# Hybrid decoder layer on one core: sink heads' values on two column halves with divided probabilities, 17 early U products, and an earlier place for a tile's exponential on ScalarE

## What is computed

```
proj = x @ w_in
fox  = forgetting attention, 8 heads x 64, causal
swa  = sliding window (128), 8 query heads, 2 key/value heads x 64, rotary, a sink logit per head:
       p = softmax([scores, sink])[..., :-1];  o = p @ v
x = LayerNorm(ALPHA * x + concat(fox, swa) @ w_out)
per token, per head (8): q = x @ w_query; scores of 2 x 128 sub keys; top 16 of each; top 16 of the sums
       g = softmax(best);  h = gelu(expert_u[idx] . x);  y = sum (g * h) * expert_v[idx]
x = LayerNorm(ALPHA * x + y)
```

## Time and profile before

| what | value |
|---|---|
| runs | 2673.73, 2677.02, 2678.19 us (median 2677.02) |
| the profiled execution, its own time | 2682.55 us |
| its span | 2680.7 us |
| PE busy | 2532.4 us, 94% |
| DVE busy | 2277.8 us, 85% |
| ACT, POOL busy | 904.8 us (34%), 1320.4 us (49%) |
| mean granted clock of PE | 0.983 |

### The profile page before, as it was taken

How to read it: one execution, slowest core, us unless ns; L and a number is a source line. 1 busy time by engine, 2 the same in 40 slices (tenths; PEclk the granted TensorE clock), 3 DMA queues, 4 the chain that set the end, 5 groups by cost and what they waited for, 6 DMA issues and landing times.

```text
span 2680.7 us, 45230 instructions
## 1 busy us (share of the span) xinstructions
PE 2532.4 (94%) x16925; PEld 1644.2 (61%) x17115; DVE 2277.8 (85%) x4525; ACT 904.8 (34%) x1602; POOL 1320.4 (49%) x864
## 2 busy tenths in 40 slices
PE   8999979999988888999999999999999999999996
PEld 5566546599877766564564665664664665664652
DVE  3666656669899998788998998998999999999998
ACT  2344345411144556332232232332332332332324
POOL 2110010100044441467777776776676776777762
PEclk9999979999999999999999999999999999999998
DMA  5100323310024477999999999999999999999995
GB/s 220 39 17 17 113 88 130 134 56 27 27 76 128 139 221 247 368 405 375 368 379 367 373 386 365 365 387 367 340 384 375 362 366 379 360 383 368 370 321 220
DMA packets 283584, 697.89 MB, mean 260 GB/s; under 512 B 31192, under 2 KB 113624, under 8 KB 277088
## 3 DMA queue, kind: packets, MB, share of 16 engines
q0 software_dynamic: 110592, 402.70, 39.6%
q1 hardware_dynamic: 170176, 284.77, 29.8%
q10 hardware_dynamic: 2592, 7.47, 0.8%
HBM read 631.51 MB, written 61.24 MB: 258 GB/s over the span
## 4 chain that ended last, share of the span: by engine, by line
PE 44%; DVE 15%; issue 9%; DMA 7%; POOL 2%; ACT 1%; DVEq 0%; SPq 0%; ACTq 0%; POOLq 0%
PE h_psum L1742 18%; PE o_psum L2225 12%; PE g_psum L2225 8%; PE r_t_psum L1203 4%; DMA early<-v_blocks,pick_index 3%; DVE rt_hot L1641 3%; DMA early<-u_rows,pick_index 2%; POOL early L1749 2%; DVE rt_top_u L1486 2%; PE h_psum L1250 1%; DVE early L2066 1%; DVE wide L2070 1%; DVE rt_top L1484 1%; DVE rt_hot L1651 1%; DVE rt_scores L1488 1%
## 5 line engine op out<-in xcount | busy, mean ns | idle before, releaser
L1742 PE MATMUL h_psum<-early 128*128 128x384 bf16 x5448 | 759.0, 299 | 1.2 <-DVE early L1732 0.9
L1742 PEld LDWEIGHTS h_psum<-early 128*128 128x128 bf16 x5448 | 532.5, 98 | 225.4 <-issue 2.1
L1749 POOL DMA_INDIRECT early<-u_rows,pick_index x320 | 466.8, 1459 | 203.1 <-DVE dots L2066 117.6
L1749 POOL DMA_INDIRECT early<-v_blocks,pick_index x320 | 462.6, 1446 | 192.6 <-DVE wide L2070 112.7
L2225 PE MATMUL o_psum<-v_split,w_split 128*128 128x512 bf16 x2293 | 538.4, 379 | 1.4
L2070 DVE SCALAR_TENSOR_TENSOR wide<-early,dots,wide 128x1024 f32<-128x1024 f32 x320 | 405.8, 1280 | 31.5 <-DMA early<-v_blocks,pick_index 28.7
L2066 DVE CUSTOM_DVE_ANT_0 early<-early,wide 128x1024 f32<-128x1024 f32 x320 | 388.1, 1221 | 38.2 <-DMA early<-u_rows,pick_index 35.5
L2225 PEld LDWEIGHTS o_psum<-v_split,w_split 128*128 128x128 bf16 x2304 | 225.7, 98 | 272.4 <-issue 1.1
L2225 PE MATMUL g_psum<-v_split,w_split 128*128 128x512 bf16 x1400 | 344.7, 380 | 17.3 <-DVE wide L2058 4.2
L1944 ACT ACTIVATE v_split<-early 128x512 bf16<-128x512 f32 x256 | 159.4, 624 | 327.7 <-PE o_psum L2225 311.5
L2225 PEld LDWEIGHTS g_psum<-v_split,w_split 128*128 128x128 bf16 x1536 | 150.0, 98 | 176.3 <-issue 12.0
(11 more groups left out here) (235 smaller groups left out, 3224.8 us busy)
## 6 DMA issues: line engine op xcount, KB each, us to landing
early<-v_blocks SPq DMA_DIRECT2D x256, 256.0 KB, 6.3
early<-u_blocks SPq DMA_DIRECT2D x114, 512.0 KB, 7.1
gates<-wide SPq DMA_DIRECT2D x16, 2048.0 KB, 9.7
gate<-gates SPq DMA_DIRECT2D x32, 1024.0 KB, 9.5
early<-w_query SPq DMA_DIRECT2D x8, 1024.0 KB, 5.6
gates_late<-wide SPq DMA_DIRECT2D x4, 2048.0 KB, 8.0
gate<-gates_late SPq DMA_DIRECT2D x32, 256.0 KB, 14.6
early<-w_fox SPq DMA_DIRECT2D x4, 1536.0 KB, 6.5
```

Of the source, the lines that this page charges most:

```text
L1742: mm = pe.matmul(bank(half)[:, 0:width * P], u_split[:, k, part, c], xs[:, first:first + width, xpart, c, :], start=(c == 0 and part == 0 ...
L1749: pool.indirect_dma_start(row, None, source, bass.IndirectOffsetOnAxis(ap=pick_index[:, tile, at:at + 1], axis=0)).then_inc(arrived, 16)
```

## The change

Three edits, and a fourth that follows from the first:

1. In the mix phase the values are made with the 64 columns of values as weights and the turned probabilities moving, a head on either half of the array's columns, so the output arrives turned; `turn_out` and `scale_out` are gone. In their place DVE's `normalise(n)` divides the probabilities before PE turns them: `turn_probs(n)` now waits for `normed` instead of `exp_done`. `normalise(n+1)` stands behind `norm` in DVE's step n.
2. 17 blocks of U products are early instead of 14: three steps of routing hold 32 pieces instead of 16. The early blocks are 6 + 7k instead of 6 + 9k.
3. ACT's `softmax(t-1)` stands behind the second group of scores of tile t instead of the third, and `softmax(0)` inside tile 1 instead of behind it.

```diff
 PRE_AHEAD = 4
-PRE_PIECES = ((0,) * 8 + (1,) * 2 + (2,) * 2 + (3,) * 2 + (4,) * 1 + (0,) * 1,) * (DENSE - 2) + (
+PRE_PIECES = ((0,) * 4 + (1,) * 3 + (2,) * 4 + (3,) * 1 + (4,) * 2 + (5,) * 2,) * (DENSE - 2) + (
     (5,) * 16, (3,) * 8 + (0,) * KD)
...
 PRE = PRE_AHEAD + (sum(map(sum, PRE_PIECES)) + sum(PRE_TURNED)) // PIECES
-PRE_BLOCKS = tuple(6 + 9 * k for k in range(PRE))
+PRE_BLOCKS = tuple(6 + 7 * k for k in range(PRE))
 UPS = tuple(b for b in range(N_KEYS) if b not in PRE_BLOCKS)
...
-                    pe.wait_ge(exp_done, n + 1)
+                    pe.wait_ge(normed, n + 1)
                     if n > 0:
...
                         pe.wait_ge(out_copied, n)
-                    for g in range(2):
-                        cols = slice(HEAD_DIM * g, HEAD_DIM * g + HEAD_DIM)
-                        for b in range(width // P):
-                            at = (2 * g + b) * P
-                            mm = pe.matmul(o_psum[:, 0, cols], probs_t[:, at:at + P],
-                                           sv_rows[:, first // P + b, cols], start=(b == 0), stop=(b == width // P - 1))
+                    for b in range(width // P):
+                        for g in range(2):
+                            dims, at = slice(HEAD_DIM * g, HEAD_DIM * g + HEAD_DIM), (2 * g + b) * P
+                            mm = pe.matmul(o_psum[dims, :], sv_rows[:, first // P + b, dims],
+                                           probs_t[:, at:at + P], start=(b == 0), stop=(b == width // P - 1))
                     mm.then_inc(values_done, 1)
-
-                def turn_out(n):
-
-                    pe.wait_ge(out_scaled, n + 1)
-                    pe.transpose(o_psum[:, 1], o_rows[:, :], ident).then_inc(out_turned, 1)
...
                         turn_probs(n)
-                    if 0 < n <= units:
-                        turn_out(n - 1)
                     if n + 1 < units:
...
                     t, j = n // PAIRS, n % PAIRS
-                    dve.wait_ge(out_turned, n + 1)
+                    dve.wait_ge(values_done, n + 1)
                     if j == 0 and t >= 2:
                         dve.wait_ge(mix_done, t - 1)
-                    dve.tensor_copy(near[:, t % 2, 0, j], o_psum[:, 1]).then_inc(out_high, 1)
+                    dve.tensor_copy(near[:, t % 2, 0, j], o_psum[:, :]).then_inc(out_high, 1)
                     dve.wait_ge(out_high, n + 1)
-                    dve.tensor_tensor(near[:, t % 2, 1, j], o_psum[:, 1], near[:, t % 2, 0, j], ALU.subtract
+                    dve.tensor_tensor(near[:, t % 2, 1, j], o_psum[:, :], near[:, t % 2, 0, j], ALU.subtract
                                       ).then_inc(out_copied, 1)
...
-                def scale_out(n):
-
-                    k = n % 2
+                def normalise(n):
+
+                    k, width = n % 2, window(n)[3]
                     dve.wait_ge(exp_done, n + 1)
...
                     dve.reciprocal(row_sum[:, k], row_sum[:, k]).then_inc(inv_made, 1)
-                    dve.wait_ge(values_done, n + 1)
                     dve.wait_ge(inv_made, n + 1)
                     for g in range(2):
-                        cols = slice(HEAD_DIM * g, HEAD_DIM * g + HEAD_DIM)
-                        scaled = dve.tensor_scalar(o_rows[:, cols], o_psum[:, 0, cols], row_sum[:, k, g:g + 1], None,
-                                                   ALU.mult)
-                    scaled.then_inc(out_scaled, 1)
+                        row = probs[:, k, g * 256:g * 256 + width]
+                        scaled = dve.tensor_scalar(row, row, row_sum[:, k, g:g + 1], None, ALU.mult)
+                    scaled.then_inc(normed, 1)
...
                 maxima(0)
+                normalise(0)
                 for n in range(STEPS):
...
                         maxima(n + 1)
-                    if n < units:
-                        scale_out(n)
                     if n >= NORM and (n - NORM) % PAIRS < 3:
                         norm((n - NORM) // PAIRS, (n - NORM) % PAIRS)
+                    if n + 1 < units:
+                        normalise(n + 1)
...
                         copy_scores(t, n)
-                        if t >= 2 and n == 2:
+                        if t >= 1 and n == 1:
                             softmax(t - 1)
...
                             copy_pre(2 * (t - 2) + n // 2, n % 2)
-                    if t == 1:
-                        softmax(0)
                 for d in range(1, DENSE - 1):
...
                 step(DENSE - 1, more=False)
```

More of the change, by code:

```diff
@@ L733, in mix_phase @@
         probs_t = sb("probs_t", [P, 4 * P])
-        o_rows = sb("o_rows", [P, P])
         neg_max, row_sum, sink_exp = sb("neg_max", [P, 2, 2]), sb("row_sum", [P, 2, 2]), sb("sink_exp", [P, 2, 2])
@@ L740, in mix_phase @@
         t_psum = ctx.enter_context(nc.psum_tensor("mx_t_psum", [P, 4 * P], F32))
-        o_psum = ctx.enter_context(nc.psum_tensor("mx_o_psum", [P, 2, P], F32))
+        o_psum = ctx.enter_context(nc.psum_tensor("mx_o_psum", [P, P], F32))
         ln_in, keys_in, sets_in = sem("ln_in"), sem("keys_in"), sem("sets_in")
@@ L747, in mix_phase @@
         exp_done, probs_turned, turn_copied = sem("exp_done"), sem("probs_turned"), sem("turn_copied")
-        sum_step, inv_made, values_done, out_scaled = sem("sum_step"), sem("inv_made"), sem("values_done"), sem("out_scaled")
-        out_turned, out_high, out_copied = sem("out_turned"), sem("out_high"), sem("out_copied")
+        sum_step, inv_made, normed, values_done = sem("sum_step"), sem("inv_made"), sem("normed"), sem("values_done")
+        out_high, out_copied = sem("out_high"), sem("out_copied")
         eps_set, mix_done, summed, stats_done = sem("eps_set"), sem("mix_done"), sem("summed"), sem("stats_done")
```

## The result

| | median, us | ratio to before, 95% interval |
|---|---|---|
| before | 2676.68 (6 runs, 2673.73 to 2679.75) | |
| after | 2685.27 (6 runs, 2677.57 to 2692.37) | 1.0032 [1.0017, 1.0047] |

The change makes the kernel 8.6 us slower, against 13 us forecast; the median lies inside the forecast's own range of 2684 to 2697, at its lower end. The profiled execution of after took 2682.23 us, 3 us under its median, and that of before took 2682.55, 6 us over its own. The two spans (2680.4 and 2680.7 us) therefore differ by only 0.3, and the whole of the two traces can't be compared. Stretches of them can. I cut the span at four events: PE's first turn in the mix phase, the first query product, the first turn of picks, and the first U product in bf16.

The account below looks back on a forecast made before the run. PE was taken to bound the kernel, with DVE close behind in the experts. Mix +26, clock +3, exponential 0, pieces +1 and experts -17 gave +13 us: 2690 against a 2677.02 median, own range 2684 to 2697.

Parts of the forecast that it names:

- What bounds the mix phase after: Mix phase: turns wait for DVE's division about 1.5 to 2 us in three steps of four; phase +26 us.
- The rival on the other side: Mix phase: LayerNorm stages 0 and 2 fit beside ACT's exponentials; mix +7, total 2668 us; chance 0.10.
- The size of that chain: Mix phase: scores, maxima, exponential, stage and division lengthen a tile from 21.55 to 25.39 us, plus 3.84.
- the first six steps: Start of the mix phase: steps without LayerNorm stages take 5.14 us each instead of about 4.8, +2.
- The column halves: Mix phase, values' products: PE stops 0.42 us ahead of them and gains about as much back, worth 0.
- the drain: Mix phase, values on column halves: a change of mode drains the array, taken to agree with the idle 0.42 us.
- The clock, +3: Mix phase: gaps of about 2 us on PE may lower its granted clock, costing 3 us.
- the case: Mix phase, clock rival: the clock falls after every gap, +22 instead of +3, total 2709 us; chance 0.08.
- The exponential: Routing's first part: DVE's 8.3 us wait for it goes, but its wait for PE's scores grows; worth 0.
- The early pieces in routing, +1: Routing's steps: 48 more pieces mostly hidden; five behind the last slot delay the next picks, +1, bounds 0 to 27.
- The experts, -17: Expert phase: three fewer U products of 6.52 us, part lost to waits; -17 us, range -13 to -19.6.

Follow-up runs that it names:

- e4: Changed kernel with DVE's division of the next unit's probabilities ahead of the LayerNorm's stage instead of behind it; 2674.53 us, ratio to before 0.9996.
- e9: e5 plus, in steps with stage 1, ACT's square root ahead of the copy of the turned probabilities; 2652.48 us, ratio to before 0.9912.
- e5: Changed kernel with the scores of unit n+1 ahead of the turn of unit n on PE; 2663.91 us, ratio to before 0.9954.
- e6: Changed kernel with both the scores ahead of the turn and the division ahead of the LayerNorm's stage; 2673.30 us, ratio to before 0.9986.
- e3: Kernel before with only the exponential of a tile's best scores one place up; 2676.76 us, ratio to before 0.9999.
- e1: Mix phase's edit alone, with early blocks, pieces and the exponential's place as in before; 2695.49 us, ratio to before 1.0073.
- e2: Kernel before with only the 17 early blocks instead of 14 and the changed kernel's table of pieces; 2667.19 us, ratio to before 0.9963.
- e8: Changed kernel with the mix phase of before, keeping 17 early blocks and the exponential's earlier place; 2667.30 us, ratio to before 0.9961.
- e10: e8 with ACT's root ahead of the copy of the turned probabilities; 2671.69 us, ratio to before 0.9984.

## Why the prediction was right, and where it was off

- **What bounds the mix phase after.** Right. The turn waits for DVE's division in three steps of four, by 1.8 to 2.1 us, and e4 shows the LayerNorm's stages 0 and 2 in that chain: taken out, steps of 6.62 and 6.22 become 5.28 and 4.98. In the step with stage 1 it is ACT's root with its tables, as forecast: e9 takes them out of the way, and 6.49 becomes 4.89. The rival on the other side (the stages fit beside the exponentials) is wrong by the same rows.
- **The size of that chain.** Forecast 6.73, 6.61, 6.47 and 5.58 us; measured 6.62, 6.50, 6.22 and 5.40. The largest part of the excess is in the division, laid at 1.08 to 1.13: from 469.17 to 470.13 it is 0.96. Per tile +3.2 instead of +3.84; with the first six steps (+1.45, forecast +2) the phase grows by 21.3, not 26. This term was over-sized by 5 us.
- **The column halves.** PE's own step is 4.67 in e5, e6 and e9, forecast 4.72, and the values' weight loads are the 1.01 us read from rows 5. But the reading that PE stops for 0.42 us ahead of such products is wrong. That is idle time of the weight loads alone; by the products' rows above, the halves save 0.25 us and cost 0.09 in front, some 0.16 us a step, not 0. So that idle time is not evidence for the drain, as the prediction took it.
- **The clock, +3.** Wrong: 0 in this kernel. The mean granted clock is 1.00 from 373 to 573 us, with all 19 waits in it. In e6 the case occurs; see below.
- **The exponential.** Right. e3 is the same within 0.1%, and the wait moved as the earlier trace rows had it.
- **The early pieces in routing, +1.** The place was right (0.95 us for the picks, several times), the size was low: over the kernels with the same mix phase, R2 is 322.2 on average in after, e4, e5, e6 and e9 against 319.4 in the one trace of e1, so +2.8. I counted one wait of the three steps; the trace has four, 3.8 us in all, against one of 0.9 in e1.
- **The experts, -17.** The nine kernels with 17 early blocks have 1602.5 us on average (1597.7 to 1607.0), the three with 14 have 1617.4 (1615.3 to 1619.6): -15. DVE's waits for gathered rows stayed:

```profile
L2213 PE MATMUL g_psum<-v_split,w_split 128*128 128x512 bf16 x1536 | 372.8, 379 | 11.2 <-DVE wide L2046 5.0 <-DVE w_split L2020 3.4 <-DVE v_split L2031 2.8
```

```profile
L2054 DVE CUSTOM_DVE_ANT_0 early<-early,wide 128x1024 f32<-128x1024 f32 x320 | 387.6, 1221 | 37.3 <-DMA early<-u_rows,pick_index 30.3 <-issue 3.5 <-DMA wide<-x_rows 1.7
```

PE's idle time ahead of these products is 11.2 us against 17.3 in this pair. The prediction read all 17.3 as waits for DVE; the row names DVE for 11.1 of them. The 4.5 us by which 15 falls short of three times 6.52 aren't located.

The terms as measured are +21.3, 0, 0, +2.8 and -15, in all +9, and the time moved by 8.6. The mix phase and the clock were laid 5 and 3 us too high, the pieces and the experts 2 us each too low; that these cancel in part is luck. One further difference was not in the sum at all. In every kernel with the old mix phase, DVE stops twice in R2 in front of a tile's best scores with nothing in the profile that releases it; in none of the seven with the new one. In before and in e2:

```profile
811.29 3.19 DVE L1484 MAX8 rt_top<-rt_scores 128x8 f32<-128x128 f32 x16 [2.14 <-issue]
```

```profile
L1484 DVE MAX8 rt_top<-rt_scores 128x8 f32<-128x128 f32 x128 | 25.6, 297 | 7.0 <-issue 7.0
```

This fits R2 being 2 to 5 us shorter with the new mix phase (e1 against e3 and before; the early kernels among themselves), and e1's 18.6 us against 21. The stops are also longer with 17 early blocks (5.8 to 7.0 us in e2, e8 and e10, 3.9 and 4.1 in e3 and before), which is most of what R2 lost in e2. Counted in, the end of the stops brings the sum to about +6, inside the interval of 4.6 to 12.6 us.

The pages have one more difference at this place, the packets of the DMA queue q14, of the kind "instruction". In before and the other four kernels with the old mix phase, and in after and the other six with the new one:

```profile
q14 instruction: 88, 0.72, 0.1%
```

```profile
q14 instruction: 77, 0.63, 0.1%
```

In before, three packets of q14 fall from 807 to 816 us, around the first stop, and three from 881 to 889, around the second. In after there are none from 820 to 845 us, around the same best scores (829.82). So the stops go with transfers of instructions. That these cause them, and why the mix edit removes them, no run varies: it stays open.

## What to carry to other kernels

An edit that takes work off the bounding engine can still lose when it puts a step into the chain between two of that engine's own instructions: write that chain down, from the last product to the next one that needs it, with everything that stands in between in program order on the other engines. Here it was enough to start the chain earlier (scores ahead of the turn) and to move ScalarE's root into its idle time, which turned +8.6 us into -24.3, of which -9.8 are the early blocks (e8). The same move of the root gained nothing where its input came late, so each such move is to be read against the arrival of its inputs.

Whether the edit itself is worth having isn't shown: no run has the old form with the scores first. By rows 2 its step without waits is 4.93 us, so a tile could come to 4 x 4.93 + 0.86 = 20.58 us as an estimate, as long as e9's.

## What the runs showed of the hardware

**The clock and waits of 2 us.** In the changed kernel the weight loads of the turns wait 2.06 and 2.09 us. The products themselves stand idle for less, 1.57 us at the first of them, and the granted clock stays at its upper level of 2.4 GHz:

```profile
470.18 0.66 PE L825 MATMUL mx_t_psum<-ident_sb,mx_probs 128*128 128x128 f32 x4 [1.57 <-DVE mx_probs L930]
```

```profile
467.10:470.20 3.10, 1.53 (x10) 0.53 (x7) 2.89 (x9) 0.52 (x3) 0.00 (x0) 1.00 1.03 349
470.20:472.00 1.80, 1.80 (x12) 1.11 (x13) 0.58 (x3) 1.10 (x2) 0.00 (x0) 1.00 1.00 400
```

In e6, a wait of the products of 1.78 us (at 425.46) is followed by a stretch with a granted clock of 0.63, between the levels of 1.2 and 2.4 GHz, another of 1.77 us (at 450.45) isn't:

```profile
426.00:430.00 4.00, 3.78 (x20) 2.25 (x19) 1.79 (x7) 3.05 (x9) 0.00 (x0) 0.63 0.56 179
```

```profile
450.45:454.00 3.55, 3.50 (x24) 2.14 (x26) 2.19 (x9) 2.05 (x8) 0.00 (x0) 1.00 0.37 148
```

The step with the drop took 9.23 us instead of 7.54, so one drop costs 1.7. Of e6's six waits of 1.77 to 1.78 us in this place two were followed by a drop; of the changed kernel's 19 of 1.33 to 1.60 us none was. Equal waits in the same place of a loop gave both, so such a cost is to be carried as a bound and not per wait.

**A table load needs no data.** In e9 the load for the root (450.25 to 451.53) runs before the moments that the root waits for have arrived (451.90), and so it hides in the wait. The Trainium skill, page "ScalarE: Activation LUTs", section "What ACT_TABLE_LOAD costs", describes the load as an instruction of its own, which agrees with its own row of 1.28 us here.
